# Other places in SBUF for two groups of tensors of a one-core transformer block

## The reference

```python
cond = jax.nn.silu(c)
mod = cond @ w_ada + b_ada                         # 2048 x 18432, nine rows of 2048
u = _modulate(_rmsnorm(h, norm1_g), sh1, sc1)
h = h + 0.5 * gt1 * _swiglu(u, ffn1_w_in, ffn1_w_out)
u = _modulate(_rmsnorm(h, norm2_g), sh2, sc2)
h = h + gt2 * _hybrid_mixer(u, ...)                # sliding window attention and an mLSTM, gated
u = _modulate(_rmsnorm(h, norm3_g), sh3, sc3)
h = h + 0.5 * gt3 * _swiglu(u, ffn2_w_in, ffn2_w_out)
return _rmsnorm(h, final_g)
```

## The kernel before

| tensor | bytes in a partition |
|---|---|
| h | 16,384 |
| raw, and lo in the same bytes | 32,768 |
| hi | 16,384 |
| act_hi, act_lo | 16,384 each |
| hid_hi, hid_lo, pad, gt_row, fin_row | 16,384 + 16,384 + 4,096 + 8,192 + 8,192 = 53,248 |
| proj, gates, from the same first byte | 34,880 + 32,768 = 67,648 |
| ada_w, over the attention scratch (s_sb, p_t, q_st, q_t, k_g, mq_t, w_sb, a_t) | 16,384 |
| ada_acc, over r_row and dgm | 8,192 |
| buf_a and buf_b, over k_t, xpad, rope_t and over par_in, bada_in | 8,192 |
| ident, ones, tri, mask, dg and the small tables, to ang | 6,528 with padding |

## Time and profile before

### The profile page before, as it was taken

The page is one execution under the profiler, slowest core; times in us unless marked ns, Lnnn a source line. Parts: engine busy times, 40 slices in busy tenths (PEclk is TensorE's granted clock), DMA queues, the critical chain, the costliest instruction groups (busy, mean ns, idle before and its releaser), DMA issues.

```text
span 2296.5 us, 27170 instructions
## 1 busy us (share of the span) xinstructions
PE 2144.0 (93%) x9729; PEld 1769.2 (77%) x9729; DVE 1485.1 (65%) x1600; ACT 952.3 (41%) x1172; POOL 2.0 (0%) x12
## 2 busy tenths in 40 slices
PE   0569999999999998999999999989999999999997
PEld 0458888888888886788788878768887888888876
DVE  5767767676675777768555588777765544554545
ACT  1214443344334444444555554444433344434443
POOL 0000000000000000000000000000000000000000
PEclk9979999999999998999999999999999999999999
DMA  7879877887777886786545467767874555555544
GB/s 260 304 259 333 290 254 273 281 291 276 256 256 240 283 268 234 270 295 205 163 149 163 148 243 271 269 224 270 282 252 151 197 187 197 183 191 194 188 160 146
DMA packets 235956, 537.21 MB, mean 234 GB/s; under 512 B 11488, under 2 KB 13792, under 8 KB 235488
## 3 DMA queue, kind: packets, MB, share of 16 engines
q1 hardware_dynamic: 235872, 536.08, 67.7%
HBM read 533.94 MB, written 2.10 MB: 233 GB/s over the span
## 4 chain that ended last, share of the span: by engine, by line
PE 88%; DVE 4%; DMA 4%; ACT 1%; issue 1%; SPq 0%; DVEq 0%; ACTq 0%
PE pa L524 14%; PE pb L524 14%; PE pb L525 14%; PE pb L526 14%; PE pa L525 14%; PE pa L526 14%; DMA ada_w<-in_w_ada_dram 3%; PE pm L551 2%; DVE ada_acc L1218 1%; DVE lo L1189 1%; PE px L536 1%; DMA h<-in_x_dram 0%; DMA raw<-in_w_in_dram 0%; ACT hi L879 0%; PE pr L764 0%
## 5 line engine op out<-in xcount | busy, mean ns | idle before, releaser
L1189 DVE TENSOR_TENSOR lo<-raw,hi 128x1024 fp32r<-128x1024 f32 (+1 forms) x744 | 883.2, 1194 | 658.3 <-ACT hi L879 657.6
L879 ACT CAST hi<-raw 128x1024 fp32r<-128x1024 f32 (+1 forms) x744 | 763.8, 1029 | 1193.0 <-PE pa L526 560.2
L524 PE MATMUL pa<-hi,act_hi 128*128 128x512 f32 (+1 forms) x1056 | 418.4, 396 | 20.0 <-issue 6.4
L525 PE MATMUL pa<-lo,act_hi 128*128 128x512 f32 (+1 forms) x1056 | 411.4, 390 | 0.0
L524 PE MATMUL pb<-hi,act_hi 128*128 128x512 f32 x1024 | 404.4, 395 | 7.2 <-DVE lo L1189 7.1
L526 PE MATMUL pa<-hi,act_lo 128*128 128x512 f32 (+1 forms) x1056 | 411.1, 389 | 0.0
L526 PE MATMUL pb<-hi,act_lo 128*128 128x512 f32 x1024 | 400.0, 391 | 0.0
L525 PE MATMUL pb<-lo,act_hi 128*128 128x512 f32 x1024 | 399.9, 391 | 0.0
L1218 DVE SCALAR_TENSOR_TENSOR ada_acc<-ada_w,cond,ada_acc 128x1024 f32<-128x1024 f32 x271 | 345.0, 1278 | 16.0 <-DMA ada_w<-in_w_ada_dram 15.0
L524 PEld LDWEIGHTS pa<-hi,act_hi 128*128 128x128 f32 x1056 | 200.7, 190 | 67.4 <-issue 16.1
L526 PEld LDWEIGHTS pa<-hi,act_lo 128*128 128x128 f32 x1056 | 200.8, 190 | 41.3
(11 more groups left out here) (231 smaller groups left out, 1265.9 us busy)
## 6 DMA issues: line engine op xcount, KB each, us to landing
raw<-in_ffn_w_in_dram SPq DMA_DIRECT2D x176, 1024.0 KB, 5.1
ada_w<-in_w_ada_dram SPq DMA_DIRECT2D x288, 512.0 KB, 5.7
raw<-in_ffn_w_out_dram SPq DMA_DIRECT2D x64, 1024.0 KB, 5.1
raw<-in_w_in_dram SPq DMA_DIRECT2D x64, 1024.0 KB, 5.1
raw<-in_ffn_w_out_dram SPq DMA_DIRECT2D x32, 768.0 KB, 4.6
raw<-in_w_out_dram SPq DMA_DIRECT2D x16, 1024.0 KB, 5.1
raw<-in_w_att_up_dram SPq DMA_DIRECT2D x8, 1024.0 KB, 5.1
raw<-in_w_mlstm_up_dram SPq DMA_DIRECT2D x8, 1024.0 KB, 5.1
```

The costliest lines, as they stand in the source:

```text
L524: pe.matmul(ps, a_hi[:, k0 + kk, tok], w_hi, start=start and kk == 0, stop=False)
L525: pe.matmul(ps, a_hi[:, k0 + kk, tok], w_lo, start=False, stop=False)
L879: act.copy(hi[:, (2 * j + half) % 4, 0:n, 0:w], raw[:, j % RING, 2 * half:2 * half + n, 0:w])\
L1189: dve.tensor_tensor(lo[:, j % RING, s, 0:w], raw[:, j % RING, s, 0:w], hi[:, (2 * j + half) % 4, 0:n, 0:w].bitcast(F32), ALU.subtract)\
```

## The change

The five tensors of the first `inner` block, and proj and gates that lie over them, are allocated last, after ang, instead of directly after act_lo. What they overlay, and all else in the kernel, is the same text. So ada_w now starts at the byte at which hid_hi and proj started, and all tensors from ada_w to ang move down by 67,648 bytes; hid_hi, hid_lo, gt_row, fin_row, proj and gates move up by 39,296 bytes.

```diff
@@ -179,14 +179,6 @@
         hi = sb("hi", [P, RING, 2, NC], F32R)
         act_hi = sb("act_hi", [P, KD, T], F32R)
         act_lo = sb("act_lo", [P, KD, T], F32R)
-        with ExitStack() as inner:
-            hid_hi = inner.enter_context(nc.sbuf_tensor("hid_hi", [P, KD, T], F32R))
-            hid_lo = inner.enter_context(nc.sbuf_tensor("hid_lo", [P, KD, T], F32R))
-            pad = inner.enter_context(nc.sbuf_tensor("pad", [P, 1024], F32))
-            gt_row = inner.enter_context(nc.sbuf_tensor("gt_row", [P, D], F32))
-            fin_row = inner.enter_context(nc.sbuf_tensor("fin_row", [P, D], F32))
-        proj = sb("proj", [P, TT, OG])
-        gates = sb("gates", [P, TT, 2 * D])
 
         def shared(*groups):
 
@@ -232,6 +224,14 @@
         pos_i = sb("pos_i", [P, TT], I32)
         ang = sb("ang", [P, 8, TT, HALF])
 
+        with ExitStack() as inner:
+            hid_hi = inner.enter_context(nc.sbuf_tensor("hid_hi", [P, KD, T], F32R))
+            hid_lo = inner.enter_context(nc.sbuf_tensor("hid_lo", [P, KD, T], F32R))
+            pad = inner.enter_context(nc.sbuf_tensor("pad", [P, 1024], F32))
+            gt_row = inner.enter_context(nc.sbuf_tensor("gt_row", [P, D], F32))
+            fin_row = inner.enter_context(nc.sbuf_tensor("fin_row", [P, D], F32))
+        proj = sb("proj", [P, TT, OG])
+        gates = sb("gates", [P, TT, 2 * D])
 
         pa = psum("pa", [P, TT, NC])
```

## The result

The changed kernel took 2312.62 us (median of 4 runs, 2311.49 to 2314.91), the kernel before 2296.74 us beside it (4 runs, 2295.8 to 2298.21). The ratio is 1.0072, 95% interval 1.0058 to 1.0084: 15.9 us slower, outside the forecast range. The engines' lists hold the same instructions in the same order as before, 27,170 of them.

A forecast was written before the change was run, and what follows sets the result against it. TensorE was taken to bound the kernel (matmuls busy 93% of the span, 88% of the chain on TensorE). Five terms of 0 left the median of the runs before, 2295.9 us, with a range of 2290 to 2301 us.

The forecast's parts named there:

- number 1: 2,496 matmuls with hid_hi or hid_lo as weights, 565 us of the path: change 0, pitch staying 0.226 us.
- The slower rival: Weight loads of hid_hi and hid_lo outlast the matmul pitch; 10 ns past it gives 2320.9 us (+1.1%); chance 0.06.
- Steps 2 to 5: L1218 on VectorE, ScalarE evacuations, TensorE's ada_acc columns and buf_b transposes, ada_w loads: each taken as 0 change.

The follow-up runs named there:

- a_gap128: The changed kernel with 128 bytes left free ahead of the first moved tensor, hid_hi at byte 154,240: 2299.16 us, ratio to the kernel before 0.9994.
- b_gap384: The kernel before with 384 bytes left free ahead of hid_hi, which so starts at byte 115,200: 2315.02 us, ratio 1.0068.
- b_act224: The kernel before with 224 bytes left free ahead of act_hi: 2351.40 us, ratio 1.0234.
- b_act192: The kernel before with 192 bytes left free ahead of act_hi: 2316.89 us, ratio 1.0083.
- b_act384: The kernel before with 384 bytes left free ahead of act_hi, raw and hi staying: 2348.43 us, ratio 1.0214.

## Why the prediction was wrong

**The step that failed is number 1**, "Matmuls with hid_hi or hid_lo as weights ... Change: 0". It rested on a comparison of act_hi with hid_hi in the kernel before. That comparison varied the region and held the offset, because every tensor between h and hid_lo is a multiple of 16,384 bytes long and so all start alike within 256 bytes. The sizes stood in the table of the code; what was missing was to ask in which bits the tensors compared differ, and which the change alters: 39,296 bytes up is 128 within 256. Measured: 5.6 ns for each of 2,496 matmuls, 14.0 us, shown by taking it away alone (a_gap128) and by making it alone (b_gap384).

**The slower rival** named the right instructions and the wrong mechanism: it wanted loads longer than the pitch, with 38 ns to spare. The loads stayed at 188 ns and the pitch grew all the same. A load that seems hidden by its duration is not thereby free of effect on what runs beside it. At 2.5 us for each ns of pitch, as it priced them, 5.6 ns give the 14 us. It got 0.06.

**Steps 2 to 5 held.** L1218 has 1280 ns against 1278, ScalarE's evacuation into buf_a 1021 against 1017, the transposes of buf_b 273 against 272, the lone loads of ada_w 22.0 GB/s per busy engine against 21.7. That the order of instructions and the waits stay as they are held too. What the place of an operand can alter was taken for nothing but each instruction's own duration; the prediction's last sentence kept open that it could hang "on which two tensors are touched at once", which is what happened, but within one engine.

On this the Trainium skill, TensorE: Matmul & The Clock Gate, section Step-by-step: what each phase is for, says that the moving operand and the weights come through two independent read ports, so that loading the next weights takes no bandwidth from the running matmul. At an equal offset within 256 bytes, 226.7 ns, nothing here speaks against it, though no run left the loads out. At other offsets the measurement decides against it: shifting the loaded tensors against the moving ones gave 228.9 to 234.3 ns for the same instructions.

**What stays open.** That the offset is the cause is shown; the mechanism behind it is not: what in the chip makes the weights' place count against the moving operands', why the period is 256 bytes, why 192 is milder than 64, and why raw's offset costs more than hi's. Other engines are not the partner as far as the trace goes: in the changed kernel the steps with hid weights average 232 to 233 ns whether or not VectorE or ScalarE has an instruction running beside them, 232.6 ns in the 474 steps with no DMA packet under way, and 232.9 ns in the 57 steps with none of the three. But no run took those engines' traffic away. Offsets finer than 32 bytes, other matmul shapes and other types were not tried.

## What to carry to other kernels

Where 128 x 512 fp32 matmuls like these stream without a pause, give the weights and both moving tensors the same offset within 256 bytes, and keep it when tensors are added or moved: a gap of 128 bytes was worth 14 us here, and the same fault on all large matmuls 50 us. Every small tensor allocated ahead of a matmul operand can break it, so lay the operands out first. And when a change is only one of place, compare places that differ in the bits that the change alters, the low ones too; a pair that agrees in them proves nothing.

## What the runs showed of the hardware

The distance between starts of 128 x 512 matmuls was 226.7 ns with weights and moving operands at equal offset within 256 bytes, and 228.9 to 234.3 ns at the seven other multiples of 32, at a granted clock of 1.00, with the loads' own median at 188 ns (187 in b_act224). The slow streams have rhythms of their own: steps that repeat after three matmuls (b_act192), as the kernel's three products do, but also after two (b_act384) or seven (the changed kernel), which no loop of the kernel does. At one and the same distance, 128, two rhythms occur in one execution. In b_act384 the block of hid weights that began at 351 us repeats after seven steps at 232.3 ns, and the one at 622 us after two, 229 and 238 ns in turn, at 233.3; in the changed kernel the block at 350 us took the second kind and the later long ones the first. So 1 ns between two pitches at distance 128 says nothing of the kernels.
